# Lower weight parts on GpSimd in pieces of 512 columns

## The reference

```python
def first_block(x, ...):                      # two layers
    p = einsum('bsd,dc->bsc', x, w_in[l])     # 1024 -> 2488 columns
    (c_q, c_kv, k_r, m_q, m_k, m_v, m_o, m_g, s_z, s_xbc, s_dt) = split(p)
    heads = concat(mla(c_q, ...), mlstm(m_q, ...), ssd(s_z, s_xbc, s_dt, ...))
    x = layernorm(ALPHA * x + heads @ w_out[l])
    x = layernorm(ALPHA * x + moe(x))
def second_block(x, ...):                     # two layers
    proj = rms_norm(x) @ w_in[l]              # 1024 -> 3912 columns
    ...  # heads are normed and rotated; an indexer scores keys and keeps the best
    x = x + concat(moba, diff, dsa) @ w_out[l]
    x = x + (silu(h2 @ w_gate[l]) * (h2 @ w_up[l])) @ w_down[l]
```

## Time and profile before

| | |
|---|---|
| time, median of 3 runs (lowest, highest) | 2541.86 us (2539.83, 2544.74) |
| profiled execution: its time, its span | 2543.53 us, 2541.4 us |
| TensorE busy | 2362.8 us, 93% of the span |
| VectorE busy | 1756.0 us, 69% |
| ScalarE busy | 1322.0 us, 52% |
| GpSimd busy | 596.5 us, 23% |
| granted TensorE clock, mean | 0.968 |
| lower parts on GpSimd (L253) | 49 instructions, 221.4 us |
| lower parts on VectorE (L253, stream buffers) | 29 instructions, 55.9 us |

### The profile page before, as it was taken

One profiled execution on the slowest core, in us unless ns is written; L12 is line 12 of the kernel. 1 busy time (PEld: TensorE's weight loads), 2 busy tenths in 40 slices (PEclk: granted clock), 3 DMA queues, 4 the chain that ended last, 5 costly groups with the idle time before them and its releaser, 6 DMA issues. The chain is left out here.

```text
span 2541.4 us, 37054 instructions
## 1 busy us (share of the span) xinstructions
PE 2362.8 (93%) x14184; PEld 1975.8 (78%) x14184; DVE 1756.0 (69%) x2775; ACT 1322.0 (52%) x2660; POOL 596.5 (23%) x333
## 2 busy tenths in 40 slices
PE   7999987997999988987998899999999989999999
PEld 7866876777866766766786689998887856899987
DVE  1756757874756757876698769984256986799942
ACT  3547616763547626765756644443157476444421
POOL 2401305771401305771460010000034500100000
PEclk9999988998999988998998999999999989999999
DMA  4210028983210019983120113323231202033221
GB/s 162 74 50 18 1 84 327 354 318 130 74 51 18 1 51 353 356 300 126 67 91 10 58 67 106 107 95 107 70 109 67 84 1 92 34 119 114 100 82 68
DMA packets 54990, 285.80 MB, mean 112 GB/s; under 512 B 13216, under 2 KB 13216, under 8 KB 28704
## 3 DMA queue, kind: packets, MB, share of 16 engines
q1 hardware_dynamic: 45600, 266.65, 29.2%
q0 software_dynamic: 9216, 16.80, 1.7%
HBM read 275.02 MB, written 25.17 MB: 118 GB/s over the span
## 5 line engine op out<-in xcount | busy, mean ns | idle before, releaser
L253 POOL TENSOR_TENSOR weights_lo<-weights_raw,weights_hi 128x2048 fp32r<-128x2048 f32 (+4 forms) x49 | 221.4, 4519 | 686.7 <-issue 356.6
L264 PE MATMUL ps<-x_operands,weights_hi 128*128 128x256 f32 x1232 | 349.4, 284 | 7.4 <-DVE weights_lo L2037 6.8
L266 PE MATMUL ps<-x_operands,weights_lo 128*128 128x256 f32 x1232 | 348.3, 283 | 0.0
L265 PE MATMUL ps<-x_operands,weights_hi 128*128 128x256 f32 x1232 | 345.9, 281 | 0.0
L215 ACT ACTIVATE weights_hi<-weights_raw 128x2048 fp32r<-128x2048 f32 (+4 forms) x80 | 136.8, 1710 | 301.7 <-PE ps L266 288.1
L264 PEld LDWEIGHTS ps<-x_operands,weights_hi 128*128 128x128 f32 x1232 | 231.3, 188 | 10.1 <-DVE weights_lo L2037 9.9
L265 PEld LDWEIGHTS ps<-x_operands,weights_hi 128*128 128x128 f32 x1232 | 233.8, 190 | 0.0
L266 PEld LDWEIGHTS ps<-x_operands,weights_lo 128*128 128x128 f32 x1232 | 230.9, 187 | 0.0
L264 PE MATMUL ps<-weights_hi,attn_ht_hi 128*128 128x512 f32 (+2 forms) x576 | 203.8, 354 | 5.0 <-DVE weights_lo L253 2.3
L265 PE MATMUL ps<-weights_lo,attn_ht_hi 128*128 128x512 f32 (+2 forms) x576 | 200.8, 349 | 0.0
L266 PE MATMUL ps<-weights_hi,attn_ht_lo 128*128 128x512 f32 (+2 forms) x576 | 200.5, 348 | 0.0
(11 more groups left out here) (529 smaller groups left out, 6278.8 us busy)
## 6 DMA issues: line engine op xcount, KB each, us to landing
weights_raw<-in_stream SPq DMA_DIRECT2D x96, 1024.0 KB, 4.8
weights_raw<-in_expert_gu SPq DMA_DIRECT2D x34, 1024.0 KB, 9.3
expert_raw<-in_expert_gu SPq DMA_DIRECT2D x30, 1024.0 KB, 9.5
expert_raw<-in_expert_down SPq DMA_DIRECT2D x18, 1024.0 KB, 8.4
weights_raw<-in_expert_down SPq DMA_DIRECT2D x14, 1024.0 KB, 8.2
weights_raw<-in_stream SPq DMA_DIRECT2D x12, 960.0 KB, 4.7
ffn_raw<-in_stream SPq DMA_DIRECT2D x10, 1024.0 KB, 4.9
weights_raw<-in_stream SPq DMA_DIRECT2D x8, 700.0 KB, 9.4
```

The source lines that it names most:

```text
L253: eng.tensor_tensor(lo[:, 0:n], self.env.raw[:, u % self.RAW, 0:n], hi[:, 0:n].bitcast(F32), ALU.subtract).then_inc(self.lo_ready, 1)
L264: nc.tensor.matmul(out, a[0], b[0], start=start, stop=False, **more)
L265: nc.tensor.matmul(out, a[0], b[1], start=False, stop=False, **more)
L266: return nc.tensor.matmul(out, a[1], b[0], start=False, stop=stop, **more)
```

## The change

`make_lo` gets a width. With it the lower part of a unit is made by several instructions over that many columns each, and the semaphore rises with the last. The GpSimd callers pass 512; VectorE's keep one instruction for each unit, the default. The experts' own weights (L2521) and the halves that VectorE makes elsewhere have functions of their own and stay as they are. `transpose_stage`, which is also touched, is called without `ahead` in this kernel, so the line there does nothing.

```diff
+POOL_PIECE = 512
...
-    def split_lo(self, eng, u):
+    def split_lo(self, eng, u, width=UNIT):
         if not self.lo_split <= u < len(self.sources):
             return
         self.lo_split = u + 1
-        self.make_lo(eng, u)
-
-    def make_lo(self, eng, u):
+        self.make_lo(eng, u, width)
+
+    def make_lo(self, eng, u, width=UNIT):
 
         eng.wait_ge(self.hi_ready, u + 1)
         n = int(np.prod(self.sources[u].shape[1:]))
         hi, lo = self.split_tiles(u)
-        eng.tensor_tensor(lo[:, 0:n], self.env.raw[:, u % self.RAW, 0:n], hi[:, 0:n].bitcast(F32), ALU.subtract
-                          ).then_inc(self.lo_ready, 1)
+        for at in range(0, n, width):
+            cols = slice(at, min(at + width, n))
+            ins = eng.tensor_tensor(lo[:, cols], self.env.raw[:, u % self.RAW, cols], hi[:, cols].bitcast(F32), ALU.subtract)
+        ins.then_inc(self.lo_ready, 1)
...
                 for n in range(2):
-                    stream.split_lo(pool, jobs[0][0] + n)
+                    stream.split_lo(pool, jobs[0][0] + n, POOL_PIECE)
...
                 for n in range(jobs[1][0] + 1, N + 1):
-                    stream.split_lo(pool, n)
+                    stream.split_lo(pool, n, POOL_PIECE)
...
-                    stream.split_lo(pool, n)
+                    stream.split_lo(pool, n, POOL_PIECE)
```

More of the change, by code:

```diff
@@ L344, in _ @@
             def _(pool):
-                env.stream.split_lo(pool, ahead)
+                env.stream.split_lo(pool, ahead, POOL_PIECE)
 def weight_units(name, K, first, last, width=BANK, rows=4 * P):
```

## The result

The changed kernel takes 2547.6 us (median of ten runs, 2544.5 to 2551.7) against 2541.7 of the kernel before (ten runs): a ratio of 1.0025, 95% interval 1.0013 to 1.0037, or 5.9 us. The profiled execution took 2548.94 us (span 2546.8). The forecast was 2547.7, and 2549.3 for the profiled execution.

The account below looks back on a forecast made before the run. It took TensorE's products plus its stops in the first two blocks' four projection stages as the bound. 2 x 1.3 + 2 x 1.6 = 5.8 us gave 2549.3 profiled, 2547.7 as median; 8-in-10 range 2542.5 to 2558.

Parts of the forecast that it names:

- Where it is bound: Four projection stages last as long as TensorE's products plus its stops; it waits for GpSimd's lower parts four times, 2.2 us.
- Alternation: Between two GpSimd pieces VectorE puts one instruction; a piece holds the other up for 1.14 us.
- the distances: Sign at u9: pieces stand 1.5 us (first block) and 1.7 us (second) apart, one VectorE instruction in each gap.
- the waits in front of u9: Sign: TensorE's wait grows from 0.84 to about 2.1 us (first block) and to about 1.5 to 2 (second).
- First block, 1.3 us a layer: u9, in pieces alternating with the latents' sums of squares, ends at 109.5 instead of 108.22: 1.3 us a layer.
- the sixteen accumulations behind start 0.2 us later: First block: u8's pieces alternate with four convolution multiplies, so the accumulations behind start 0.2 us later, delaying u9.
- Second block, 1.6 us a layer: u9 ends 1.9 us later among VectorE multiplications, less 0.3 us gained in front; u4's 0.4 does not add.
- at the other units the same working leaves TensorE no stop: Units other than those worked out do not stop TensorE; the narrowest, second block's u5, has a few tenths to spare.
- (1) starved pieces: First block: convolution work keeps u8's pieces out, TensorE stalls 10.5 us; some 19.6 us in all, 2561.5 us; chance 0.15.
- (2) GpSimd keeps its turn: The next piece goes before waiting VectorE, so units cost only fixed parts: 2.1 us, 2544.0, no measurable change; chance 0.17.
- (3) entry at the first gap: First block's u9 alternates with the accumulations from 100.6, removing TensorE's 0.84 us wait: 1.5 us, 2543.4; chance 0.05.
- (4) faster: VectorE's stalls shrink, ScalarE's passes come earlier, all five stops on GpSimd and ScalarE vanish: 5.1 us, 2536.8; chance 0.05.

Follow-up runs that it names:

- e2: Changed kernel with u9 of the first block and u4, u9 and u11 of the second left whole: 2543.2 us, ratio 1.0009 to the kernel before.
- e3: Changed kernel with pieces only at u9 of the first block and u4, u9, u11 of the second, others whole: 2552.7 us, ratio 1.0051 to the kernel before.
- e4: Changed kernel, but VectorE waits for u9 before the latents' sums of squares (first block) and first rotation (second): 2545.6 us, ratio 1.0019 to the kernel before.
- e5: Changed kernel with pieces of 256 columns instead of 512: 2569.2 us, ratio 1.0114 to the kernel before.

## Why the prediction was right, step by step

**Where it is bound.** Right: the stops of TensorE at lower parts grew by 5.2 us, the time by 5.9 (by the interval 3.3 to 9.4). GpSimd's share and VectorE's did not decide it.

**Alternation.** Right in kind: one VectorE instruction in each gap, at u9 in both blocks. e2 and e3 show that only units with a stop pay. In e4 the second block's u9 takes 5.06 us. So of the 2.05 us by which 6.65 exceeds a whole unit's 4.60, some 1.6 come from VectorE's instructions in front and in the gaps, and 0.45 are the fixed parts, which u4 pays too. e5 shows that the loss grows with the number of gaps. Of the signs named, the distances came (1.43 and 1.71 us for 1.5 and 1.7), the waits in front of u9 came smaller: 1.40 us for 2.1 in the first block, 1.12 for 1.5 to 2 in the second. Which of the two goes first differed between the blocks. In the second, a piece was in front each time: the rotations of 0.7 us take 1.64 to 1.78 behind a piece. In the first, the accumulations stayed in front, as in the earlier trace rows: u9's first piece, asked for at 100.25, lasts until 104.81, through five further accumulations.

**First block, 1.3 us a layer: too large, it was 0.43.** (u8 lasts 0.59 us longer, u10 0.14 less.) The step that failed is "the sixteen accumulations behind start 0.2 us later": they start 0.36 earlier (92.98 against 93.34). I added the multiplies to the pieces one after the other, 1.14 + 0.46; the rows show pieces 1.43 apart, so beside the forecast's own 1.14 for a piece a multiply costs GpSimd 0.29, and the last multiply ends just behind the last piece. u9 then begins 0.36 earlier, and its sums of squares cost 0.29 a gap rather than 0.35: 108.82 instead of the 109.5 forecast.

**Second block, 1.6 us a layer: right to u9, too small behind it.** u4 took 5.02 instead of 4.60, its stop grew by 0.41, as forecast, and u9 absorbed it, as forecast. u9 was asked for 0.3 us earlier in the stage, as allowed, its gaps were 1.71 us apart, and it began 1.43 us later in the stage (first of the two layers), against 1.6 forecast. The step that failed is "at the other units the same working leaves TensorE no stop": u11 stops it 0.49 us, and with the products around it 0.8 a layer. In the trace of before, u11 met the small tables and held the first of them for 4.24 us. In pieces, VectorE comes through u8 to u10 0.8 us earlier in the stage, u11 is asked for 1.4 us later in it (behind the stop at u9), the tables are done at 1282.79, and the rotations of 0.7 us meet u11's pieces. I had put the changed instructions beside the old positions of the others. GpSimd at u11 and VectorE's instruction that meets it, in the timeline, before and then after (u11 of after stands above):

```profile
1282.23 4.63 POOL L253 TENSOR_TENSOR weights_lo<-weights_raw,weights_hi 128x2048 fp32r<-128x2048 f32 x1 [1.64 <-ACT weights_hi L215]
1282.76 4.24 DVE L3208 TENSOR_TENSOR rope_tables<-consts,vec 128x128 f32<-128x128 f32 x1
...
1282.82 1.79 DVE L3220 TENSOR_TENSOR rope_a<-proj,rope_tables 128x512 f32<-128x512 f32 x1
```

So 2 x 0.43 + 2 x 2.1 = 5.1 us stand where 2 x 1.3 + 2 x 1.6 = 5.8 stood: errors of -1.7 and +1.0 that cancel in part. That the median came within 0.1 us of the forecast is luck, by these errors and by the scatter.

**Rivals.** (1) starved pieces: u8's pieces alternate with the multiplies, 1.43 us apart, no stop near 94. (2) GpSimd keeps its turn: excluded by the rows at u9. (3) entry at the first gap: 4.6 us until the first piece is through. (4) faster: the stops on ScalarE's pass are still 2.9 us.

## What to carry to other kernels

Cutting an instruction on one of two engines that hold each other up was not free here. It gave VectorE a turn in every gap of u9, and the cut work ended later by part of one VectorE instruction for each gap (0.18 us of 0.41 in the first block, 0.46 of 0.69 in the second). Look up which pieces of work somebody is waiting for, leave those whole or, where it has the time, give them to the engine that does them faster (here VectorE, 2.29 us against GpSimd's 4.60 for 2048 columns), and cut only those with time to spare. When one engine gains time by a change, follow it to its next meeting with the other one, and to what the other has next in its order: twice here a stop arose two units further on.

## What the runs showed of the hardware

VectorE's instructions did not all give way alike. The convolution's accumulations kept GpSimd's request out for all that were left, 3.4 us from 100.25 to the end of the run at 103.66. The scaled latents, also scalar_tensor_tensor instructions, but four of 256 columns and then four of 128 where the accumulations have 512, let a piece in before each of the last four, which take 1.10 to 1.39 us each. Both in the timeline of the changed kernel:

```profile
122.28 6.59 DVE L967 SCALAR_TENSOR_TENSOR proj<-proj,gates_latent_ss,vec 128x256 f32<-128x256 f32 x8
...
123.79 4.93 POOL L256 TENSOR_TENSOR weights_lo<-weights_raw,weights_hi 128x512 fp32r<-128x512 f32 x4 [9.37 <-ACT weights_hi L216]
```

Four pieces take 4.93 us here, hardly more than alone (4.74 and 4.76 at u6 and u7). The number of columns alone does not decide it: the scores' accumulations of 512 columns (those at 1245.67, 1248.13 and 1249.57, 1.41 us long each where the one at 1251.02 takes 0.75) also let GpSimd's 512-column scaling in, but each of them starts 0.03 us or more after the instruction in front has ended, where the convolution's start 0.66 apart and last 0.74 each. What makes the difference (length, the waits between accumulations, operands) was not tried.

What slipped in cost GpSimd less than it lasted: 0.18 us for a sum of squares of 0.41 (1.43 apart against 1.25 alone), 0.46 for a rotation of 0.69 (1.71 against 1.25).

Stops of TensorE of 1.77 us (e3) and 2.02 (e5) in the first block were followed by a granted clock of 0.86 over the next unit, and stops of 1.95 and 3.01 in the second block (e5) by 0.87. Stops of 1.40 in the first block, and of 1.74 (e3) and 3.06 (e5) in the second, were followed by 1.00. So the length of the stop alone did not tell, and a fall cost 1.5 to 1.6 us each time.
